# Output projection of chunks 1 and 2 as seven block products, with stored low parts of the input weights

## The reference

```
mod = silu(c) @ w_ada + b_ada;  shift, scale, gate = split(mod, 3)
h = layer_norm(x) * (1 + scale) + shift
xa, ga, u, v, gb = split(h @ w_in)                    # five times 512 columns
ya = pool_mixer(xa, w_pool, pool_scale) * silu(ga)    # causal means over 2/4/8/16 tokens, minus xa
yb = gelu(u) * (tril(w_sgu) @ layer_norm(gelu(v)) + b_sgu) * silu(gb)   # chunks of 128 tokens, 4 heads
y = concat([ya, yb]) @ w_out
out = layer_norm(2 ** 0.25 * x + gate * y) * ln_g + ln_b
```

## Time and profile before

| | |
|---|---|
| median of 3 runs | 673.7 us (673.05 to 674.21) |
| the profiled execution | 673.68 us, of which the span (first to last instruction) 671.6 us |
| PE busy, matmuls | 659.8 us (98%), 3103 |
| DVE / ACT busy | 516.1 us (77%) / 235.1 us (35%) |
| DMA | 108.73 MB, mean 162 GB/s |

### The profile page before, as it was taken

The page is one execution under the profiler, slowest core; times in us unless marked ns, Lnnn a source line. Parts: engine busy times, 40 slices in busy tenths (PEclk is TensorE's granted clock), DMA queues, the critical chain, the costliest instruction groups (busy, mean ns, idle before and its releaser), DMA issues.

```text
span 671.6 us, 8845 instructions
## 1 busy us (share of the span) xinstructions
PE 659.8 (98%) x3103; PEld 551.3 (82%) x3103; DVE 516.1 (77%) x956; ACT 235.1 (35%) x307; POOL 61.7 (9%) x77
## 2 busy tenths in 40 slices
PE   8999999999999999999999999999999999999995
PEld 8888888877888888888888888888888888888884
DVE  5678898749969967766979968775977986656776
ACT  4424644316522333224722332322821333323300
POOL 2000110100002201100002201000002210000010
PEclk9999999999999999999999999999999999999999
DMA  8995643785334472288243562378343454224111
GB/s 340 365 332 233 219 153 116 163 228 189 125 111 141 126 258 86 95 116 322 96 156 100 180 248 65 106 94 332 102 148 90 162 205 159 104 79 154 52 63 62
DMA packets 34546, 108.73 MB, mean 162 GB/s; under 512 B 6573, under 2 KB 7633, under 8 KB 34514
## 3 DMA queue, kind: packets, MB, share of 16 engines
q1 hardware_dynamic: 34514, 108.31, 49.5%
HBM read 97.80 MB, written 10.50 MB: 161 GB/s over the span
## 4 chain that ended last, share of the span: by engine, by line
PE 95%; issue 2%; DVE 2%; ACT 0%; DMA 0%; POOLq 0%; POOL 0%; DVEq 0%
PE bank_b L1053 63%; PE bank_a L1053 25%; PE bank_a L1180 2%; PE bank_a L1140 1%; PE bank_b L1113 1%; PE bank_a L1171 1%; DVE w_low L656 1%; PE bank_b L1077 0%; DVE v_gelu L708 0%; PE bank_b L1171 0%; PE bank_b L1132 0%; PE bank_b L1104 0%; DMA vector_rows<-in_vectors 0%; ACT h_high L528 0%; ACT w_high L509 0%
## 5 line engine op out<-in xcount | busy, mean ns | idle before, releaser
L1053 PE MATMUL bank_b<-h_high,w_high 128*128 128x512 f32 x512 | 202.2, 395 | 0.2 <-DVE h_low L668 0.2
L1053 PE MATMUL bank_b<-h_low,w_high 128*128 128x512 f32 x512 | 199.3, 389 | 0.0
L1053 PE MATMUL bank_b<-h_high,w_low 128*128 128x512 f32 x512 | 199.3, 389 | 0.0
L661 DVE TENSOR_TENSOR w_low<-w_float,w_high 128x1024 fp32r<-128x1024 f32 x98 | 119.5, 1220 | 40.3 <-ACT w_high L518 40.2
L518 ACT ACTIVATE w_high<-w_float 128x1024 fp32r<-128x1024 f32 x98 | 103.4, 1056 | 130.5 <-DMA w_float<-in_w_units 57.2
L1053 PEld LDWEIGHTS bank_b<-h_high,w_high 128*128 128x128 f32 x512 | 96.2, 188 | 20.2 <-issue 1.1
L1053 PEld LDWEIGHTS bank_b<-h_high,w_low 128*128 128x128 f32 x512 | 96.1, 188 | 20.1
L1053 PEld LDWEIGHTS bank_b<-h_low,w_high 128*128 128x128 f32 x512 | 96.2, 188 | 19.5 <-issue 0.5
L461 POOL TENSOR_TENSOR z_rstd<-z_var_eps,minus_half 128x1 f32<-128x1 f32 x16 | 22.0, 1377 | 361.8 <-DVE z_var_eps L905 351.9
L1053 PE MATMUL bank_a<-w_high,y_high 128*128 128x512 f32 x128 | 49.9, 390 | 0.2 <-issue 0.2
L1053 PE MATMUL bank_a<-w_high,y_low 128*128 128x512 f32 x128 | 49.8, 389 | 0.0
(11 more groups left out here) (180 smaller groups left out, 934.0 us busy)
## 6 DMA issues: line engine op xcount, KB each, us to landing
w_float<-in_w_units SPq DMA_DIRECT2D x90, 512.0 KB, 3.4
x_norm<-in_x SPq DMA_DIRECT2D x16, 512.0 KB, 4.5
z<-in_x SPq DMA_DIRECT2D x16, 512.0 KB, 5.2
out<-z SPq DMA_DIRECT2D x15, 512.0 KB, 4.8
z<-in_mod_units SPq DMA_DIRECT2D x12, 512.0 KB, 9.1
x_norm<-in_x_channels SPq DMA_DIRECT2D x12, 512.0 KB, 15.0
w_float<-xa_units SPq DMA_DIRECT2D x12, 512.0 KB, 3.5
mod_spare<-in_mod_units SPq DMA_DIRECT2D x6, 512.0 KB, 8.6
```

Of the source, the lines that this page charges most:

```text
L661: vec.tensor_tensor(wL[:, n % S_SLOTS, :], w_float(c, n), wH[:, n % S_SLOTS, :].bitcast(F32), ALU.subtract).then_inc(w_low, 1)
L1053: last = mm(bank, wl if n == 2 else wh, ml if n == 1 else mh, start=start and n == 0, stop=stop and n == 2)
```

## The change

**Fewer products.** In chunks 1 and 2 (FAST) y is taken as 2x2 blocks (token halves by the yp and ys rows) and `w_out` as 2x2 blocks, and the output is made by seven block products with sums of blocks as operands, in place of eight. A block product is two units of 12 matmuls each (`fast_unit`), so the output stretch has 14 units (20 to 33), again of 512 KB.

**Sums of weights.** For each of the four row groups q of `w_out`, SP loads two units (`prep_load`), DVE multiplies them by `gate_rows` (`gate_weights`, 2 instructions of 128x1024) and makes four sums (`sum_weights`, 128x512), and SP stores seven pieces of 256 KB (`prep_store`) to `out_units`, from where chunks 1 and 2 load their output weights. q = 0 and 1 stand in chunk 0 (n = 23 to 27), q = 2 and 3 in chunk 1 (n = 2 to 9).

**Sums of y.** At each group's YS place DVE makes four sums of 128x256 (`sums_of_y`); the low parts come from them. The sums s3 and s4 are split late, at n = 25 to 28 (`late_low`).

**z.** A product is read from PSUM straight into z, by 16 instructions per chunk (`add_parts`, two or four after each product, in the order of PARTS; the last product at n = 0 of the next chunk), statistics follow (`z_stats_of`). Products 4, 5 and 6 are accumulated on banks that still hold earlier ones, so PE waits until those have been read.

**Low parts.** In chunk 0 SP stores each input unit's low part (`store_low`, 20 times 512 KB); in chunks 1 to 3 ACT issues a load of it into `w_low` in front of its `w_high` (20 per chunk), and DVE splits no input unit there.

**Slots and tables.** Half of the output units of chunks 1 and 2 land in `v_gelu`, so four slots serve there. The x tables of chunks 1 and 2 stand earlier. The loop over chunks 1 and 2 is written out.

The diff, cut: the tables, then SP (`store_low`, `prep_store`), ACT (in `split_high`), DVE (`gate_weights`, `sum_weights`, `add_parts`) and PE (`fast_unit`).

```diff
+FAST = (1, 2)
+PRODUCTS = 7
+FAST_UNITS = IN_UNITS + 2 * PRODUCTS
+PARTS = ((0, 0, 0, 0), (0, 1, 1, 0), (1, 2, 2, 0), (1, 3, 3, 0), (2, 4, 0, 0), (2, 5, 1, 0), (3, 6, 2, 1), (3, 7, 3, 1),
+         (4, 4, 0, 1), (4, 5, 1, 1), (5, 6, 0, 1), (5, 7, 1, 1), (6, 4, 2, 1), (6, 4, 2, 0), (6, 5, 3, 1), (6, 5, 3, 0))
+READ_IN = {IN_UNITS + 3 + 2 * i: i for i in range(PRODUCTS - 1)}
+LATE_IN = {25: 0, 26: 1, 27: 2, 28: 3}
+PREP_LOAD_IN = {(0, 18): 0, (0, 19): 1, (0, 27): 2, (1, 6): 3}
+GATE_IN = {(0, 23): 0, (0, 26): 1, (1, 2): 2, (1, 8): 3}
+SUMS_IN = {(0, 24): 0, (0, 27): 1, (1, 4): 2, (1, 9): 3}
+PREP_STORE_IN = {(0, 25): 0, (1, 1): 1, (1, 6): 2, (1, 11): 3}
+FAST_X_STATS_IN = {8: 0, 9: 1, 10: 2, 11: 3}
+FAST_X_ROWS_IN = 12
+FAST_X_CENTRE_IN = {16: (0, 1), 17: (2, 3), 18: (4, 5), 19: (6, 7)}
+FAST_H_IN = {22: (0,), 23: (1,), 24: (2,), 26: (3,), 28: (4,), 29: (5,), 30: (6,), 32: (7,)}
...
+        def landing(c, n):
+            if c == 0 and n in XA_ALONE:
+                return None
+            if c in FAST and n >= IN_UNITS and (n - IN_UNITS) % 4 >= 2:
+                return F_SLOTS + n % F_SLOTS
+            return n % F_SLOTS
...
+            def store_low(n):
+                sp.wait_ge(w_low, max(n + 1, len(EARLY)))
+                stored = low_stored[n % S_SLOTS] if n >= V_UNITS else v_low_stored if n else v0_low_stored
+                sp.dma_start(low_units[n], w_of(0, n)[1].bitcast(F32)).then_inc(stored, 16)
...
+            def prep_store(q):
+                sp.wait_ge(prep_ready, q + 1)
+                zero, one, (t12, t4) = prep_tile(q, 0), prep_tile(q, 1), prep_sums(q)
+                for i, half_unit in enumerate((zero[:, 0:T], t4, zero[:, T:], t12[:, 0:T], t12[:, T:], one[:, 0:T],
+                                               one[:, T:])):
+                    cut = slice(q % 2 * T, (q % 2 + 1) * T)
+                    sp.dma_start(out_units[i, q // 2][:, cut], half_unit).then_inc(out_stored, 16)
...
-                nc.scalar.activation(wH[:, n % S_SLOTS, :], w_float(c, n), ACT.Copy).then_inc(w_high, 1)
+                if low_loaded(c, n):
...
+                    nc.scalar.dma_start(w_of(c, n)[1].bitcast(F32), low_units[n])\
+                        .then_inc(low_landed[(base(c) + n) % S_SLOTS], 16)
+                nc.scalar.activation(w_of(c, n)[0], w_float(c, n), ACT.Copy).then_inc(w_high, 1)
...
+            def gate_weights(q):
...
+                for half in range(2):
+                    rows = prep_tile(q, half).rearrange("p (b n) -> p b n", b=2)
+                    gate = gateB[:, half * HALF:(half + 1) * HALF].rearrange("p (o n) -> p o n", o=1)
+                    dve.wait_ge(prep_landed[half], (q + 1) * 16)
+                    done = vec.tensor_tensor(rows, rows, gate.broadcast_to([P, 2, T]), ALU.mult)
+                prep_steps.then(dve, done)
+            def sum_weights(q):
...
+                if 0 < q < G - 1:
+                    dve.wait_ge(out_stored, q * PRODUCTS * 16)
+                prep_steps.then(dve, vec.tensor_tensor(t12[:, 0:T], b12, b11, ALU.subtract))
+                prep_steps.then(dve, vec.tensor_tensor(t12[:, T:], b22, t12[:, 0:T], ALU.subtract))
+                vec.tensor_tensor(t4, b21, t12[:, T:], ALU.subtract)
+                vec.tensor_tensor(b12, b22, b12, ALU.subtract).then_inc(prep_ready, 1)
+            def add_parts(c, i):
+                nth = FAST.index(c) * len(PARTS)
+                dve.wait_ge(unit_done, base(c) + IN_UNITS + 2 * i + 2)
+                for p, (product, bank, j, half) in enumerate(PARTS):
...
+                    if earlier:
+                        dve.wait_ge(part_read, nth + earlier[0] + 1)
+                        ins = vec.tensor_tensor(z[:, j, cut], psum, z[:, j, cut], ALU.add)
+                    else:
+                        dve.wait_ge(z_landed[j], (c + 1) * 16)
+                        ins = vec.scalar_tensor_tensor(out=z[:, j, cut], in0=z[:, j, cut], scalar=ALPHA, in1=psum,
+                                                       op0=ALU.mult, op1=ALU.add)
+                    ins.then_inc(part_read, 1)
...
+            def fast_unit(c, w, i, r):
...
+                if r == 0 and i >= 4:
+                    pe.wait_ge(part_read, nth * len(PARTS) + 2 * i - 2)
+                bank0 = (0, 2, 4, 6, 4, 6, 4)[i]
+                for qq in range(2):
+                    q = 2 * r + qq
...
+                    for t in range(2):
...
+                        done = product(psum, high[:, at, cut], low[:, at, cut], w[0][:, block], w[1][:, block],
+                                       start=(i < 4 and q == 0), stop=(q == G - 1), skip_group_check=(i > 3))
```

More of the change, by code:

```diff
@@ L228, in wait, with run_chunks, units, base @@
                 eng.wait_ge(s, value)
-        def run_chunks(eng, chunk):
-            chunk(0, True, False)
-            with eng.Fori(1, CHUNKS - 1) as c:
-                chunk(c, False, False)
-            chunk(CHUNKS - 1, False, True)
+        def run_chunks(chunk):
+            for c in range(CHUNKS):
+                chunk(c, c == 0, c == CHUNKS - 1)
+        def units(c):
+            return FAST_UNITS if c in FAST else UNITS
+        def base(c):
+            return sum(units(i) for i in range(c))
+        def own(c, n):
+            return (c, n) if n < units(c) else (c + 1, n - units(c))
+        def low_loaded(c, n):
+            return c > 0 and n < IN_UNITS
+        def lows(c, n):
+            return n + 1 if c == 0 else UNITS + sum(units(i) - IN_UNITS for i in range(1, c)) + n - IN_UNITS + 1
+        def low_loads(c, n):
+            before = sum(1 for i in range(1, c) for u in range(IN_UNITS) if (base(i) + u) % S_SLOTS == (base(c) + n) % S_SLOTS)
+            return before + n // S_SLOTS + 1
+        def classic(c):
+            return sum(1 for i in range(c) if i not in FAST)
         def places(first):
@@ L376, in chunk @@
             def chunk(c, first, last):
-                for n in range(V_UNITS if first else 0, UNITS):
+                _, x_rows_in, _, _ = x_tables(c)
+                for n in range(V_UNITS if first else 0, units(c)):
                     if first and n == V_UNITS + 2:
@@ L385, in chunk @@
                         load_w(c, n + 2 * AHEAD)
+                    if first and n in (5, 9, 10):
+                        for unit in {5: (4, 5, 6, 7, 0), 9: (1,), 10: (2, 3)}[n]:
+                            store_low(unit)
+                    if first and FIRST_LOOP <= n + AHEAD < IN_UNITS:
+                        store_low(n + AHEAD)
                     if first and n in (12, 13):
@@ L416, in chunk @@
                             .then_inc(rows_stored, 16)
-                        for i in range(TILES):
+                    if not last and x_rows_in <= n < x_rows_in + TILES:
+                        for i in (n - x_rows_in,) if c in FAST else (range(TILES) if n == x_rows_in else ()):
                             sp.dma_start(xT[:, 2 * i:2 * i + 2, :], x_channels[c + 1][:, 2 * i:2 * i + 2, :])\
                                 .then_inc(xT_landed[i], 16)
-                    if not last and n == 17:
+                    if not last and n == x_rows_in + 1:
                         sp.wait_ge(rows_stored, (c + 1) * 32)
@@ L591, in chunk @@
                 sgu_after, mix_in, ys_in = places(first)
-                for n in range(FIRST_LOOP if first else 0, IN_UNITS + 1 if last else UNITS):
+                _, _, _, h_in = x_tables(c)
+                for n in range(FIRST_LOOP if first else 0, IN_UNITS + 1 if last else units(c)):
                     if not (last and n in LAST_SPLITS_IN):
@@ L639, in chunk @@
                                 .then_inc(gate_ready, 1)
-                    if not last and IN_UNITS <= n < IN_UNITS + 4:
-                        for k in range(2 * (n - IN_UNITS), 2 * (n - IN_UNITS) + 2):
+                    if not last and n in h_in:
+                        for k in h_in[n]:
                             h_evacuate(c + 1, k)
-            run_chunks(act, chunk)
+            run_chunks(chunk)
         @block.vector
@@ L941, in chunk @@
                     first_branches(c)
-                for n in range(FIRST_LOOP if first else 0, IN_UNITS + 1 if last else UNITS):
+                x_stats_in, _, x_centre_in, h_in = x_tables(c)
+                for n in range(FIRST_LOOP if first else 0, IN_UNITS + 1 if last else units(c)):
+                    if c in FAST and n in READ_IN:
+                        add_parts(c, READ_IN[n])
                     if not (last and n in LAST_SPLITS_IN):
@@ L1321, in chunk @@
             def chunk(c, first, last):
                 sgu_after, _, _ = places(first)
-                for n in range(V_UNITS + len(EARLY_CHANNEL) if first else 0, IN_UNITS if last else UNITS):
+                for n in range(V_UNITS + len(EARLY_CHANNEL) if first else 0, IN_UNITS if last else units(c)):
                     w = w_of(c, n)
-                    pe.wait_ge(w_low, c * UNITS + n + 1)
+                    if low_loaded(c, n):
```

(4 more changed lines are left out.)

301 lines of the change are left out of this document (240 added, 61 removed).

## The result

The changed kernel takes **682.1 us** (median of 4 runs, 681.33 to 683.97) against 673.4 us before in the same session: a ratio of 1.0132, interval 1.0109 to 1.0156. It is 8.8 us slower where 7.7 us faster was forecast, and the forecast's range ended at 673.5.

A forecast was written before the change was run, and what follows sets the result against it. PE was taken as the bound, by its number of matmuls. From 673.7 us, - 10.9 (saving) + 2.5 (end of chunk 0) + 0.7 (output stretches) gave 666.0 us; forecast 664 to 668 (0.52), range 662.0 to 673.5.

The forecast's parts named there:

- The saving: PE in chunks 1 and 2: 48 fewer matmuls at 0.2267 us each, 10.9 us less.
- Rival D: Output stretches: matmuls cost more, say 0.25 us, so 674 us, no change; chance 0.05, shared with Rival C's mild end.
- The end of chunk 0: PE waits 2.5 us before chunk 1 for DVE's fourth `bank_a` read, behind work for q = 0 and 1; bounds 1.0 and 5.0.
- 2.5 us more if the stores take 2.5 us longer: End of chunk 0: sums for q = 1 wait for q = 0's seven stores; adds nothing unless these take longer.
- what makes that landing later shifts everything behind it: Chunk 0: a later landing of unit 21's weights delays the work behind it; taken as 1.5 us, between 0 and 3.
- A pause of PE of this length does not lower its clock: End of chunk 0: a pause of about 2.5 us keeps the 2.4 GHz level, judged by the trace's tail.
- The input stretches: From chunk 1 on DVE loses 20 low parts per chunk, 22.4 us of cover; loading them costs PE nothing.
- issued up to three units (16 us) ahead of its use: Input stretches: the low part's load is issued this early and lands in 3.4 us, so it costs nothing.
- The output stretches: Chunks 1 and 2: DVE nearly full, product 4 with 1.1 us to spare; PE stands 0.7 us for both.
- The transfers: Chunk 1's input stretch (108.9 us): 39.6 MB at 408 GB/s plus 12 us around the token rows just fits, 109 us.
- Rival C: Chunk 1: DMA engines set the pace, weights and low parts late; 17 us at 348 GB/s, 683 us; chance 0.11.
- Rival B: DVE sets the pace of the output stretches, each losing 1.5 to 3 us more: 669 to 672 us; chance 0.17.

The follow-up runs named there:

- e11: Changed kernel with token rows in 16-byte pieces (plain view), sums behind the `bank_a` reads, gate rows copied before unit 21's high part, x normalised earlier: 662.5 us.
- e2: Changed kernel with ACT copying the gate rows ahead of the high part of unit 21, nothing left out: 683.7 us.
- e14: Only the stored low parts of the change (eight products, no sums), with token rows in 16-byte pieces and plain view: 672.9 us, ratio 0.9988 to before.
- e4: Changed kernel without gate products and sums of weights, their loads and stores; products read plain output weights: median 673.6 us.
- e9: Changed kernel with token rows stored in 16-byte pieces and x tiles reordered so that DVE reads the rows plainly: 669.2 us.
- e12: Changed kernel with only two order edits: sums behind the `bank_a` reads, gate rows copied ahead of unit 21's high part: 675.3 us.

## Why the prediction was wrong

**The saving (10.9 us): right.** 3055 matmuls, 0.2267 us apart wherever PE does not pause at full clock, and e11 pays it out in full. Rival D is out.

**The end of chunk 0 (2.5 us): the mechanism right, a term missing.** The pause was 3.2 us, on the read that was named. But that it came near 2.5 is luck: the sums for q = 1 began at 199.06 instead of about 194.5, 4.6 us late, and hid behind PE, which came 4 us late itself; in e2, where PE came in time, the same pause is 8.4 us. The bound "2.5 us more if the stores take 2.5 us longer" named the right wait: the stores began 0.8 us later than I put them, the last of the seven was issued at 193.25, not at about 190.5, since one took 0.7 us in the queue on average instead of the earlier trace rows's 0.43, and they landed 5.8 us after it, not 3.9. What failed is the step "what makes that landing later shifts everything behind it", which I followed on DVE alone. On ACT the same landing stands in front of the copies of the gate rows, for which PE waits with no slack: before, they were over at 151.77, 0.1 us ahead of PE's start. That was 2.3 us and 1.6 at half pace. In all, what I had at 2.5 us came to 8.8 (7.15 by PE's start of chunk 1, and 1.6 at half pace behind it).

**"A pause of PE of this length does not lower its clock": wrong.** The tail, where no matmul follows, was no ground for it. Windows of the kernel after behind the two pauses, and two around a pause of 2.42 us that ends at 296.35:

```profile
154.00:160.00 6.00, 5.54 (x17) 4.46 (x18) 5.82 (x9) 1.91 (x3) 0.00 (x0) 0.72 1.02 408
202.00:206.00 4.00, 3.33 (x8) 2.70 (x9) 3.82 (x8) 1.06 (x1) 0.00 (x0) 0.60 0.96 299
290.00:296.00 6.00, 4.32 (x20) 3.23 (x18) 0.99 (x2) 2.06 (x3) 0.00 (x0) 1.00 1.02 407
296.00:300.00 4.00, 3.65 (x16) 3.07 (x17) 0.30 (x1) 0.00 (x0) 0.00 (x0) 1.00 1.01 404
```

The granted clock of 0.72 and 0.60 is a mean of both levels, some matmuls at 1.2 GHz and the rest at 2.4: 1.6 us lost each time, 4.2 in all. Around the third pause it stayed at 1.00.

**"The input stretches: nothing": wrong, and most of what was lost behind chunk 0 hangs on it.** PE's pause there was 2.2 us only. The step that failed for it is the low part's load "issued up to three units (16 us) ahead of its use": it stands behind ACT's wait for the same unit's weights (10.20 us here) and was issued at 292.99, 3.4 us before PE went on. No run issues it ahead of that wait, so what that would give is not shown. The larger fault is that the cover was counted once for everything. DVE's slack was spent on waiting for landings, and the same slack was to carry the work of the output stretch.

**The output stretches (0.7 us for both): mis-sized, 7.1 us** (4.5 and 1.0 in chunk 1, 1.6 in chunk 2). I began the count with DVE at n = 20 in step with PE. It came late, with 10.6 us of normalising still in n = 16 to 19 (16 instructions, 0.72 and 0.61 us apart in turn), and had two units of lead in a place where a unit had become half as long. Before the change, two units ahead was 10.9 us; now it is 5.4. So the place I checked (product 4's reads) was not the one that failed (the low parts of units 21 to 23).

**The transfers.** Rival C had the right place and sign and the wrong mechanism. It held that 350 GB/s would be too little. The windows on both sides of the hole show 400 to 417 GB/s, 413 in the window that follows the seven stores of sums (the last was issued by 272.7, and one took 6.5 us to land in the median); the time went into the hole that the sum had put at "12 us" and that I then let pass as harmless because a wait of 10 us had cost PE nothing. e14 and e11 settle it: without the hole the bytes of the low parts cost nothing (e14), and neither do all that the change adds (e11). Rival B (DVE sets the pace of the output stretches) was right on the engine, and its 3 to 6 us more are close to the 6.4 that the stretches took beyond my 0.7. The two were treated as alternatives, and they are one chain: hole, late high parts, idle DVE, late low parts.

**Left open**: why the runs of e4, e9 and e12 spread over 4 to 9 us and those of e11 over 0.3. Their PE leans on landings in places where e11's does not, which was not tested by itself.
